# Joining two products of a split-precision up projection into one of 512 columns, and two evictions moved

## What is computed

```python
def swiglu(x, w_in, w_out):
    gate, up = jnp.split(x @ w_in, 2, axis=-1)
    return (jax.nn.silu(gate) * up) @ w_out
# first_block, for i in range(DEPTH):       (DEPTH = 2, D_MODEL = 1024, D_FF = 2816, SEQ = 256)
        h = x + 0.5 * swiglu(rms_norm(x, norm_ffn1[i]), w_ffn1_in[i], w_ffn1_out[i])
        ...   # attention and convolution side by side, gated, w_o
        h = h + 0.5 * swiglu(rms_norm(h, norm_ffn2[i]), w_ffn2_in[i], w_ffn2_out[i])
        x = h + (p[i] @ w_pe_proj[i]) * jax.nn.sigmoid(rms_norm(h, norm_pe[i]) @ w_pe_gate[i])
# second_block, for layer in range(DEPTH):  (D_FF_2 = 4096)
        proj = rmsnorm(x, ln1_g[layer]) @ w_in[layer]
        ...   # three attentions: dilated windows, latent (MLA), differential
        x = x + mixed @ w_o[layer]
        u = rmsnorm(x, ln2_g[layer]) @ w_up[layer]
        x = x + jnp.square(jax.nn.relu(u)) @ w_down[layer]
```

## Time and profile before

| | |
|---|---|
| median of 3 runs | 1790.33 us (1789.78 to 1791.37) |
| the profiled execution's own time | 1790.14 us |
| its span | 1788.3 us |
| TensorE busy | 1775.1 us, 11422 products |
| VectorE busy | 1105.5 us |
| ScalarE busy | 893.1 us |
| mean granted clock of TensorE | 0.999 |

### The profile page before, as it was taken

One profiled execution on the slowest core, in us unless ns is written; L12 is line 12 of the kernel. 1 busy time (PEld: TensorE's weight loads), 2 busy tenths in 40 slices (PEclk: granted clock), 3 DMA queues, 4 the chain that ended last, 5 costly groups with the idle time before them and its releaser, 6 DMA issues.

```text
span 1788.3 us, 28974 instructions
## 1 busy us (share of the span) xinstructions
PE 1775.1 (99%) x11422; PEld 1616.9 (90%) x11422; DVE 1105.5 (62%) x1604; ACT 893.1 (50%) x1304; POOL 26.5 (1%) x32
## 2 busy tenths in 40 slices
PE   9999999999999999999999999999999999999998
PEld 9998898899988999888889998889898988989896
DVE  6554588765555655468776554667565556756554
ACT  5444456544444544355654443567553446745342
POOL 0000000000000000000000000000000000000000
PEclk9999999999999999999999999999999999999999
DMA  8854533554455555543345545534355543435541
GB/s 303 225 185 166 211 113 123 189 176 184 177 176 189 189 188 177 199 166 118 134 173 195 178 168 185 183 131 144 115 189 200 177 163 117 143 115 191 199 178 48
DMA packets 45852, 303.22 MB, mean 170 GB/s; under 512 B 5104, under 2 KB 6256, under 8 KB 12312
## 3 DMA queue, kind: packets, MB, share of 16 engines
q1 hardware_dynamic: 45720, 301.36, 47.8%
HBM read 300.02 MB, written 1.31 MB: 168 GB/s over the span
## 4 chain that ended last, share of the span: by engine, by line
PE 97%; ACT 1%; DVE 1%; issue 1%; POOLq 0%; POOL 0%; ACTq 0%; DVEq 0%
PE ps L469 15%; PE ps L471 15%; PE ps L470 15%; PE ps L520 14%; PE ps L521 14%; PE ps L522 14%; PE ps L542 2%; PE ps L798 2%; PE ps L616 1%; PE ps L822 1%; PE ps L627 1%; PE ps L649 1%; PE ps L807 1%; PE ps L497 0%; PE ps L495 0%
## 5 line engine op out<-in xcount | busy, mean ns | idle before, releaser
L1512 DVE TENSOR_TENSOR wlo<-raw,whi 128x1024 fp32r<-128x1024 f32 (+4 forms) x388 | 657.1, 1705 | 415.7 <-ACT whi L1001 415.5
L1001 ACT ACTIVATE whi<-raw 128x1024 fp32r<-128x1024 f32 (+4 forms) x388 | 554.2, 1443 | 356.3 <-PE ps L471 223.8
L520 PE MATMUL ps<-x_hi,wlo 128*128 128x256 f32 x2048 | 582.1, 284 | 1.4 <-DVE wlo L1512 1.4
L521 PE MATMUL ps<-x_lo,whi 128*128 128x256 f32 x2048 | 579.5, 283 | 0.0
L522 PE MATMUL ps<-x_hi,whi 128*128 128x256 f32 x2048 | 579.5, 283 | 0.0
L520 PEld LDWEIGHTS ps<-x_hi,wlo 128*128 128x128 f32 x2048 | 393.0, 192 | 3.1 <-DVE wlo L1512 1.6
L521 PEld LDWEIGHTS ps<-x_lo,whi 128*128 128x128 f32 x2048 | 393.0, 192 | 0.5
L522 PEld LDWEIGHTS ps<-x_hi,whi 128*128 128x128 f32 x2048 | 393.0, 192 | 0.0
L469 PE MATMUL ps<-whi,hid_hi 128*128 128x512 f32 x600 | 233.9, 390 | 0.0
L470 PE MATMUL ps<-wlo,hid_hi 128*128 128x512 f32 x600 | 233.5, 389 | 0.0
L471 PE MATMUL ps<-whi,hid_lo 128*128 128x512 f32 x600 | 233.4, 389 | 0.0
(11 more groups left out here) (265 smaller groups left out, 1497.8 us busy)
## 6 DMA issues: line engine op xcount, KB each, us to landing
raw<-in_w SPq DMA_DIRECT2D x261, 1024.0 KB, 4.8
raw<-in_w SPq DMA_DIRECT2D x12, 768.0 KB, 4.2
raw<-in_w SPq DMA_DIRECT2D x14, 512.0 KB, 3.3
raw<-in_w SPq DMA_DIRECT2D x4, 576.0 KB, 3.5
raw<-in_w SPq DMA_DIRECT2D x4, 432.0 KB, 3.2
bias<-line_scratch SPq DMA_DIRECT2D x8, 192.0 KB, 10.1
h<-in_x SPq DMA_DIRECT2D x2, 512.0 KB, 5.7
out<-h SPq DMA_DIRECT2D x2, 512.0 KB, 2.7
```

Of the source, the lines that this page charges most:

```text
L520: e.matmul(o, wl, x_hi[:, c, :], start=first and n == 0 and m % 2 == 0, stop=False)
L521: e.matmul(o, wh, x_lo[:, c, :], start=False, stop=False)
L1001: e.activation(w_at(whi, j, off, n), raw[:, j % RAW, off:off + n], ACT.Copy).then_inc(s_hi, count)
L1512: e.tensor_tensor(w_at(wlo, j, off, n), raw[:, j % RAW, off:off + n], f32(w_at(whi, j, off, n)), ALU.subtract).then_inc(s_lo, count)
```

## The change

The up projection of the wide groups is formed anew. x_lo and x_hi become two halves of one tile `x`, so that for each chunk 512 columns, low part and high part of all 256 tokens, lie side by side. `wide_` issues for each block of 128 weight columns one product of 512 columns (high weights by low and high x) into a whole bank and one of 256 (low weights by high x) into the bank's upper half: within a chunk first the four wide ones and then the four narrow ones, in the next chunk the other way round. A group now takes four banks, in turn P2 with SO and G0 with G1. Groups 0 and 1 of every feed-forward keep `columns_`; in the second block these are the first two of the first half only, and the second half is not crossed any more.

The two halves of each bank are added behind TensorE: ScalarE copies the lower half to `tmp` (`lefts`, `up`), VectorE adds the upper (`parts_sum`), and gate, up and square read `tmp`. In the second block Relu becomes a copy, VectorE does maximum and square in one instruction (`square`) and ScalarE's Square becomes a copy. The down products of the first half use P2 and SO (`down_bank`). In `mixer2` on ScalarE the ticks stand ahead of the evictions of `mla_w_uq_2` and, behind those of `mla_w_ukv_2`, ahead of the split. The small product for the head biases comes two ticks earlier.

```diff
@@ -81,7 +81,7 @@
-    out += crossed(u[0], u[1]) + u[2] + u[3]
+    out += (crossed(u[0], u[1]) if hf == 0 else u[0] + u[1]) + u[2] + u[3]
@@ -175,6 +175,28 @@
+def wide(name, l, j):
+    narrow = {"ffn1": (0, 1), "ffn2": (0, 1), "up2": (0, 1)}[name]
+    if j in narrow:
+        return None
+    if name == "up2":
+        return ("P2", "SO") if j in (2, 5, 7) else (bank(name, l, 0), bank(name, l, 1))
+    return ("P2", "SO") if j % 2 == 0 else (bank(name, l, 1), bank(name, l, 0))
+def left(F, j, i):
+    return 18 * F + 2 * (j - 2) + i + 1
+def down_bank(l, hf, g):
+    return ("P2", "SO")[g] if hf == 0 else bank("up2", l, 10 + g)
@@ -248,8 +270,7 @@
-x_hi = sb("x_hi", [128, 8, 256], F32R)
-x_lo = sb("x_lo", [128, 8, 256], F32R)
+x = sb("x", [128, 8, 512], F32R)
@@ -288,10 +309,10 @@
-PS = [ctx.enter_context(nc.psum_tensor(f"ps{i}", [128, 512], F32)) for i in range(8)]
-BANKS = {"G0": (PS[0], PS[1]), "G1": (PS[2], PS[3]), "P2": (PS[4], PS[5]), "SO": (PS[6], PS[7])}
-TB = (PS[4], PS[5], PS[6])
-O = PS[7]
+PAIR = {b: ctx.enter_context(nc.psum_tensor(f"ps{b}", [128, 2, 512], F32)) for b in ("G0", "G1", "P2", "SO")}
+BANKS = {b: (p[:, 0, :], p[:, 1, :]) for b, p in PAIR.items()}
+TB = (*BANKS["P2"], BANKS["SO"][0])
+O = BANKS["SO"][1]
@@ -330,6 +351,9 @@
+x_lo, x_hi = x[:, :, 0:256], x[:, :, 256:512]
@@ -528,6 +552,50 @@
+    def wide_(spec, bks, name, l):
+        j = NUM[spec]
+        first, last = spec[2][0] == 0, spec[2][-1] == 7
+        for n, c in enumerate(spec[2]):
+            e.wait_ge(s_lo, split_value(j, n * 512))
+            e.wait_ge(s_xlo, xv(name, l, c))
+            end = last and n == len(spec[2]) - 1
+            def high():
+                for m in range(4):
+                    if first and n == 0:
+                        for s, v in free[bks[m // 2]][m % 2]:
+                            e.wait_ge(s, v)
+                    wh = w_at(whi, j, n * 512 + m * 128, 128)
+                    i = e.matmul(BANKS[bks[m // 2]][m % 2], wh, x[:, c, :], start=first and n == 0, stop=end)
+                return i
+            def low():
+                for m in range(4):
+                    wl = w_at(wlo, j, n * 512 + m * 128, 128)
+                    i = e.matmul(BANKS[bks[m // 2]][m % 2][:, 256:512], wl, x_hi[:, c, :], start=False, stop=False)
+                return i
+            if n % 2 == 0:
+                high()
+                i = low()
+            else:
+                low()
+                i = high()
+            if n == len(spec[2]) - 1:
+                i.then_inc(s_used, 1)
+            if n % 2 == 1 and n < len(spec[2]) - 1:
+                tick()
+        tick()
+    def wide_frees(bks, *when):
+        for bk, w in zip(bks, when):
+            for t in range(2):
+                free[bk][t] = [w]
@@ -572,7 +640,7 @@
-        for _ in range(8):
+        for _ in range(6):
@@ -592,10 +660,14 @@
-            if j > 1:
-                columns_(u[j][0], bank(f, l, j), f, l)
-            columns_(u[j][1], bank(f, l, j), f, l, mid=(lambda: spread(f, l)) if j == 0 else None)
-            gate_frees(j)
+            bks = wide(f, l, j)
+            if bks is None:
+                columns_(u[j][1], bank(f, l, j), f, l, mid=(lambda: spread(f, l)) if j == 0 else None)
+                gate_frees(j)
+            else:
+                wide_(u[j][0], bks, f, l)
+                wide_(u[j][1], bks, f, l)
+                wide_frees(bks, (s_gate, 11 * F + j + 1), (s_up, 11 * F + j + 1))
@@ -926,20 +998,21 @@
-            def relu_frees(j):
-                free[bks[j]] = [[(s_relu, 2 * (Q + j) + i + 1)] for i in range(2)]
-            columns_(u[0][0], bks[0], "up2", l)
+                columns_(u[0][0], bks[0], "up2", l)
-            columns_(u[1][0], bks[1], "up2", l)
+                columns_(u[1][0], bks[1], "up2", l)
-                if j > 1:
-                    columns_(u[j][0], bks[j], "up2", l)
-                columns_(u[j][1], bks[j], "up2", l)
-                relu_frees(j)
+                w = wide("up2", l, 4 * hf + j)
+                if w is None:
+                    columns_(u[j][1], bks[j], "up2", l)
+                    free[bks[j]] = [[(s_relu, 2 * (Q + j) + i + 1)] for i in range(2)]
+                else:
+                    wide_(u[j][0], w, "up2", l)
+                    wide_(u[j][1], w, "up2", l)
+                    wide_frees(w, *((s_relu, 2 * (Q + j) + i + 1) for i in range(2)))
-                bk = bks[4 + g]
+                bk = down_bank(l, hf, g)
@@ -1066,6 +1139,14 @@
+        def lefts(j):
+            for i, bk in enumerate(wide(f, l, j)):
+                out = tmp[:, (j % 2) * 1024 + i * 512:(j % 2) * 1024 + i * 512 + 512]
+                e.wait_ge(s_used, NUM[u[j][1]] + 1)
+                e.wait_ge(s_hlo, 11 * F + j - 1)
+                e.activation(two(out), PAIR[bk][:, :, 0:256], ACT.Copy).then_inc(s_left, 1)
...
+                lefts(j)
@@ -1362,13 +1444,12 @@
         tick()
         for g in range(2):
             spec = piece("mla_w_uq_2", l, (0, 1, 2), cols(g, 288))
-            use(spec, end=False)
+            use(spec)
             for t in range(2):
                 e.wait_ge(s_used, NUM[spec] + 1)
                 e.wait_ge(s_cr2, l + 1)
                 e.activation(cq[:, t, g * 288:g * 288 + 288], BANKS[bks[4 + g]][t][:, 0:288], ACT.Copy,
                              scale=sm[:, 148 + t:149 + t]).then_inc(s_out2, 1)
-            tick()
         spec = piece("mla_w_ukv_2", l, (0,), (0, 768))
         for g in range(2):
             for t in range(2):
@@ -1415,13 +1496,18 @@
-            def relu(j):
+            def up(j):
+                w = wide("up2", l, 4 * hf + j)
-                    sq = tmp[:, (j % 2) * 1024 + i * 512:(j % 2) * 1024 + i * 512 + 512]
+                    out = tmp[:, (j % 2) * 1024 + i * 512:(j % 2) * 1024 + i * 512 + 512]
-                    e.activation(sq, BANKS[bank("up2", l, 6 * hf + j)][i][:, :], ACT.Relu).then_inc(s_relu, 1)
+                    if w is None:
+                        e.activation(out, BANKS[bank("up2", l, 6 * hf + j)][i], ACT.Copy).then_inc(s_upc, 1)
+                    else:
+                        e.activation(two(out), PAIR[w[i]][:, :, 0:256], ACT.Copy).then_inc(s_upc, 1)
@@ -1429,22 +1515,20 @@
-                    e.activation(flat(F2["hid_hi"][:, 4 * j + 2 * i:4 * j + 2 * i + 2, :]), sq, ACT.Square).then_inc(s_uhi, 1)
+                    e.activation(flat(F2["hid_hi"][:, 4 * j + 2 * i:4 * j + 2 * i + 2, :]), sq, ACT.Copy).then_inc(s_uhi, 1)
-            high(NUM[u[1][0]] + AHEAD)
+                high(NUM[u[1][0]] + AHEAD)
-            relu(0)
-            high(NUM[u[1][1]] + AHEAD)
-            hid(0)
-            relu(1)
-            for j in (2, 3):
-                high(NUM[u[j][0]] + AHEAD)
+            up(0)
+            for j in (1, 2, 3):
+                if hf == 1 or j > 1:
+                    high(NUM[u[j][0]] + AHEAD)
-                relu(j)
+                up(j)
@@ -1586,12 +1670,16 @@
-        for _ in range(8):
+        for _ in range(6):
+    def parts_sum(out, bk):
+        return step(e.tensor_tensor(two(out), PAIR[bk][:, :, 256:512], two(out), ALU.add))
@@ -1603,15 +1691,27 @@
-            ps = BANKS[bank(f, l, j)]
-            e.wait_ge(s_used, NUM[u[j][1]] + 1)
+            bks = wide(f, l, j)
-            e.tensor_tensor(two(gt), two(ps[0][:, :]), rsb2, ALU.mult).then_inc(s_gate, 1)
+            if bks is None:
+                e.wait_ge(s_used, NUM[u[j][1]] + 1)
+                g_in, u_in = (b[:, :] for b in BANKS[bank(f, l, j)])
+            else:
+                e.wait_ge(s_left, left(F, j, 0))
+                v = parts_sum(gt, bks[0])
+                e.wait_ge(s_left, left(F, j, 1))
+                w = parts_sum(pr, bks[1])
+                g_in, u_in = gt, pr
+                e.wait_ge(s_dv, v)
+            e.tensor_tensor(two(gt), two(g_in), rsb2, ALU.mult).then_inc(s_gate, 1)
-            e.tensor_tensor(pr, ps[1][:, :], gt, ALU.mult).then_inc(s_up, 1)
+            if bks is not None:
+                e.wait_ge(s_dv, w)
+            e.tensor_tensor(pr, u_in, gt, ALU.mult).then_inc(s_up, 1)
@@ -2136,27 +2236,40 @@
+            def square(j):
+                w = wide("up2", l, 4 * hf + j)
+                sq = [tmp[:, (j % 2) * 1024 + i * 512:(j % 2) * 1024 + i * 512 + 512] for i in range(2)]
+                v = [None, None]
+                for i in range(2):
+                    e.wait_ge(s_upc, 2 * (Q + j) + i + 1)
+                    if w is not None:
+                        v[i] = parts_sum(sq[i], w[i])
+                for i in range(2):
+                    if w is not None:
+                        e.wait_ge(s_dv, v[i])
+                    e.scalar_tensor_tensor(out=sq[i], in0=sq[i], scalar=0.0, in1=sq[i], op0=ALU.max, op1=ALU.mult).then_inc(s_relu, 1)
-                    v = step(e.tensor_tensor(sq, sq, sq, ALU.mult))
-                    e.wait_ge(s_dv, v)
-            low(NUM[u[1][0]] + AHEAD)
+                low(NUM[u[1][0]] + AHEAD)
```

(21 more changed lines are left out.)

## The result

The changed kernel takes 1770.87 us (median, 1770.33 to 1771.66) against 1790.09 of the kernel before: a ratio of 0.9892 with a 95% interval of 0.9875 to 0.9909, so 19.2 us or 1.1% faster. Forecast were 1766.8 us and 23.5 us of gain, range 1764 to 1772.

What follows compares the result with a forecast made beforehand. TensorE, busy 1775.1 of 1788.3 us, was taken as the bound. Joined products (20.5 us) and moved evictions (3.0) sum to 23.5 us off the median of 1790.33, about 1766.8 us; forecast within 1764.5 to 1770, range 1764 to 1772.

Steps and rivals of the forecast that it cites:

- The price of a product, columns plus 13.3 ns whatever its width: TensorE's up and down stages: products of 256 columns start 120.0 ns apart, of 512 columns 226.7 ns.
- Changes of width cost nothing: TensorE's wide stages: 384 changes between 512- and 256-column products, at 0 to 0.01 us each, taken as 0.
- Copies, sums and the banks at 0: Behind TensorE in wide groups: ScalarE's copies and VectorE's sums fit, banks are free in time; cost 0.
- the splits' lead: Weight splits in wide feed-forward groups run three pieces ahead: 9.1 us of lead, bearing turns up to 12.2 us.
- The evictions, 3.0 us: Second mixers: ScalarE's reordered ticks remove TensorE's waits behind lines 1304 and 1290; 3.0 us saved, bounds 0 to 3.4.
- The sum: Whole kernel: 20.5 us from wide products plus 3.0 from moved evictions, 23.5 us gained, median about 1766.8 us.
- the 20.5 us of the joined products: Wide up projections: 1536 joined products each save one fixed part of 13.3 ns on TensorE.
- rivals, 2: Width changes (4 us), late banks (up to 4) or mixers without gain (3) leave 1768 to 1778 us; chance 0.10.
- rival 1: Wide products: the fixed 13.3 ns isn't saved, time 1783.5 to 1787.3 us; sign 0.24 us or more apart; chance 0.06.
- rival 3: Wide feed-forward groups: VectorE's turn becomes the bound and the kernel slower, 1810 us at a 13.6 us turn; chance 0.03.

Runs made afterwards that it cites:

- e1: Changed kernel with each 512-column product split back into two of 256, banks, copies, sums and moved evictions kept: 1787.91 us.
- e3: Changed kernel with sixteen wide products of a piece, then its sixteen narrow ones, the next piece the other way round: 1768.02 us.
- e7: Changed kernel with two more 128x512 VectorE instructions in every wide group of the gated feed-forwards, between sums and gate: 1771.30 us.
- e8: Changed kernel with four more 128x512 VectorE instructions in every wide group of the gated feed-forwards, between sums and gate: 1786.84 us.
- e5: Changed kernel with only the first eviction of mla_w_uq_2 behind its tick, the second ahead of it as before: 1770.01 us.

## Why the prediction was right or wrong

1. *The price of a product, columns plus 13.3 ns whatever its width.* Right. Undoing the join costs 17.0 us in e1, and 20.8 with the 3.8 for changes of width that go away at the same time: 13.6 ns for each of 1536 products (13.4 by the traces). The rule of the Trainium skill's page "TensorE: Matmul & The Clock Gate", section "Back-to-back issue gap" (2.5 ns; 3.8 us for the whole change is an estimate from it), leaves the weight loads out, as the page says, and doesn't hold for these products; the runs show 13.3 to 13.6.
2. *Changes of width cost nothing.* This step failed, and it is most of the miss. Its bounds were 0 to 4 us and I took the lower end, because the edges in the earlier trace rows agree with the plain price. But each row there is the first product only, at 0.01 us resolution, and the surcharge comes to no more than that on each of five products. It needed the sum over a run of them: 3.8 us by the rows of after, nearly the whole upper bound, 2.9 of it won back by e3. The trace of before already held it, a few rows behind those of the earlier trace rows:

```profile
140.28 0.39 PE L471 MATMUL ps<-whi,hid_lo 128*128 128x512 f32 x1
...
141.41 0.39 PE L470 MATMUL ps<-wlo,hid_hi 128*128 128x512 f32 x1
```

From 139.12 to 140.28 five products of 512 columns take 1.16 us, the next five 1.13. All twelve places of that trace where such products follow a stretch of 256-column ones show the same five distances, 27 ns more in sum.

3. *Copies, sums and the banks at 0.* Right: no wait of TensorE for any of them, and e7 hides two more instructions. The chain was well sized (10.3 for 10.5). ScalarE's busy time was added up wrongly (its terms make 6.2 us, not 6.9), but nothing rests on it. The margin behind the chain was wrong: I took the splits' lead for the cover and gave 12.2 us as the turn that it bears, and e8, at 12.37, loses 16 us, because the banks come due first.
4. *The evictions, 3.0 us.* The two waits went as described. The term was too large by 0.6 (2.4 measured), since I asked who waits for the late eviction's result and not for its bank. The bank cost some 0.5 us per layer, and e5 removes most of that; without it the evictions bring 3.2 to 3.3 us, within the bounds of 0 to 3.4.
5. *The sum.* 23.5 less 3.8 less 0.6 makes 19.1; measured 19.2. The sign and the 20.5 us of the joined products came by the stated mechanism. Of the rivals, 2 (some is given back, chance 0.10) is what occurred: its first term is the changes of width at 4 us, and 1770.87 lies in its 1768 to 1778, but outside the 1764.5 to 1770 of the forecast proper. The range to 1772 held because it had been drawn 2 us wider. The sign named for rival 1, wide products 0.24 us apart, didn't come (0.236 at most, averaged over the runs), nor that of rival 3, a wait for the low split within the up stages.

## What to carry to other kernels

Where one engine is always busy, count its instructions and multiply by the fixed part read from the distance between starts. Joining two products with the same stationary operand is worth that part if the additions behind it fit into other engines' idle time. A surcharge just below the resolution of a row has to be read over a long stretch, and a bound that comes from resolution isn't a reason for the lower end. When an eviction is moved later, look for who needs the bank as well as who needs the data.

## What the runs showed of the hardware

- At 2.4 GHz (granted clock 0.999), with weights loaded for each, products of 256 and of 512 fp32r columns start 120.0 and 226.7 ns apart, with one bank per three products or a new bank each time.
- Every product here has its own weight load, and the loads (188 ns each in the trace) lie beside the products before them; which of the two the 13.3 ns over the columns' time belongs to stays open.
- Behind 256-column products the first five 512-column ones take 233, 236, 228, 233 and 231 ns to the next start, in the changed kernel, in e3 and at the stage edges of before, and the first 256-column one behind them takes 113. That is 20 ns per pair of changes in runs of eight, 5 to 7 ns when wide and narrow alternate, and nothing further in runs of 32. Why is open.
- A VectorE instruction of 128x512 that waits for the result of the one before it starts 0.72 us after it (105.28, 105.99 and 106.72 in e7_two_more); with independent sums the next starts after 0.60 (80.78 to 81.99 for two in the changed kernel).
